# A gated-linear-attention loop on Trainium2: where GpSimd multiplies the keys and queries by their decay, and the order of products in the first late gate tile

## The chip, the cores and the metric

The kernel runs on one core of a Trainium2 chip. Its engines work side by side and meet by semaphores: TensorE (PE, matrix products into PSUM), VectorE (DVE), ScalarE (ACT), GpSimd (POOL), and SyncE (SP), which issues the DMAs. The metric is the device time of one execution in microseconds (us), as the median of several runs.

## The reference, cut to what matters

The whole program is three blocks: a convolution mixer, a gated linear attention (GLA) over 1024 tokens and 16 meta tokens, and a second block with attention and a feed-forward part. The change lies in the GLA block, whose core is this:

```
def _gla_chunk_step(S, inp):
    qc, kc, vc, gc = inp
    bc = jnp.cumsum(gc, axis=1)
    o_inter = jnp.einsum('bthd,bhde->bthe', qc * jnp.exp(bc), S)
    ...
    att = jnp.einsum('bthd,bshd,btshd->bhts', qc, kc, decay)
    o_intra = jnp.einsum('bhts,bshe->bthe', att, vc)
    b_last = bc[:, -1]
    S_new = jnp.exp(b_last)[..., None] * S + jnp.einsum(
        'bshd,bshe->bhde', kc * jnp.exp(b_last[:, None] - bc), vc)
    return S_new, o_inter + o_intra
```

After the loop the outputs are normed per head and multiplied by `silu(r)`, where `r` is a part of the product `h @ w_in`; that product with its silu is called the gate here.

## The kernel before

Numbers are float32. A product that needs the accuracy is made of three products of split operands: each operand is cut into a high part and a low part (`xh`, `xl` for the activations, `wh`, `wl` for a weight unit of 256 columns), and high times high, high times low and low times high are added in PSUM. A tile of 128 tokens by 256 columns is 8 steps over the depth times 3 = 24 matmuls (`token_tile`, its matmuls are recorded at line 354).

The GLA loop runs over `TILES`: tile 0 has the 16 meta tokens, tiles 1 to 8 have 128 tokens each (`NX` is 8). One pass c of it, on each engine in the order in which that engine's program is written:

- **TensorE** (`gla_tensor`): gate products of tile c (line 1049, spread between the others), gate logits of tile c+1 (1021), the pair scores from `arg_a` and `arg_b` (1082), the diagonal scores of tile c+1 (1060), the transposition of the decayed keys of tile c+1 (`turn_keys`, 1030), then a wait for `att_ready`, and then the output products (1096 and 1097, the second from `q_decayed`) and the state products (1104).
- **VectorE** (`gla_vector`): the state update (1275), the masked diagonal (1248), the early gate (1195), then for tile c+1 `sums` (a minimum at 1206, four running sums at 1212, one per head, a small product at 1215) and `exponents(c+1, 0)`, eight differences into `arg_a` (1226 and 1227); then `weights` of tile c, seven predicated copies of the pair scores from PSUM into `att` under a mask that lies in SBUF (1236), whose end raises `att_ready`; then `exponents(c+1, 1)`, six differences into `arg_b`.
- **ScalarE** (`gla_scalar`): exponentials, silus, squares and copies. Exponentials of the decayed keys are at 1130 (they raise `kdec_exp`), those of `arg_a` and `arg_b` at 1138, that of the decayed queries at 1154 (raises `qdec_exp`), the soft part of the gate at 1119 to 1122; the squares of the outputs stand at 1149, and the copy of the outputs out of PSUM at 1185.
- **GpSimd** (`gla_pool`): multiplies what ScalarE has exponentiated by the keys and queries: `k_decayed` (one instruction, line 1291), the eight halves of `arg_a` and the six of `arg_b` (1298 and 1299), `q_decayed` (one instruction, line 1302).

Nothing plans this order: it is that of the code. An engine that waits for a semaphore holds up all that stands behind the wait on it.

After the loop comes the late gate (`gla_gate_tensor`): 16 tiles (`EARLY`) of the last two of four gate columns' units. Its first unit, `U_R[2]`, is loaded by a DMA that SyncE issues when the last pair scores are done; VectorE then makes the high part (line 341, raises `unit_hi`) and the low part (line 343, raises `unit_ready`). The tiles use PSUM banks 4 to 7 in turn, so tile q from the fourth on waits until ScalarE has read tile q-4 (`r_left`). ScalarE (`gla_gate_scalar`) takes the silu of each tile and between them casts the high parts of later weight units (`BETWEEN`), which GpSimd completes with the low parts (line 330).

Of the kernel before, what the change touches and what calls it, by code (L numbers as in the profile page):

```python
# [5 lines left out]
ALU = mybir.AluOpType  # L6
# [5 lines left out]
P = 128  # L12
D = 1024
SEQ = 1024
META = 16
T = META + SEQ
KT = D // P
NX = SEQ // P
# [7 lines left out]
UNIT = 256  # L26
GH, GK, GV = 4, 128, 256
# [9 lines left out]
TILES = [(0, META)] + [(META + P * j, P) for j in range(NX)]  # L37
# [9 lines left out]
U_R, U_GO = (U_GR, U_GR + 1, U_GR + 2, U_GR + 4), (U_GR + 3, U_GR + 5, U_GR + 6, U_GR + 7)  # L47
# [22 lines left out]
def hybrid_block(nc, I, out):  # L70
    ctx = ExitStack()
    with ctx:
        base = (nc.sbuf_base + 31) // 32 * 32

        def at(name, shape, off, dt=F32):
            return nc.alloc_sbuf_tensor_at(name, shape, dt, offset=base + off)

        def sem(name):
            return ctx.enter_context(nc.semaphore(name))
# [22 lines left out]
        xh = at("xh", [P, KT, T], A0, F32R)  # L102
        xl = at("xl", [P, KT, T], A0 + KT * T * 4, F32R)
# [4 lines left out]
        wh = [at(f"wh{s}", [P, KT, UNIT], o, F32R) for s, o in enumerate(SLOTS)]  # L108
        wl = [at(f"wl{s}", [P, KT, UNIT], o + SLOT // 2, F32R) for s, o in enumerate(SLOTS)]
# [19 lines left out]
        qk = at("qk", [P, 2 * GH, T], Z0)  # L129
# [8 lines left out]
        k_decayed = at("k_decayed", [P, GH, P], S0 + 2 * SLOT)  # L138
# [8 lines left out]
        q_decayed = at("q_decayed", [P, GH, P], W0 + 8192 + 2048)  # L147
# [72 lines left out]
        PS = ctx.enter_context(nc.psum_tensor("PS", [P, 8, 512], F32))  # L220
# [28 lines left out]
        raw_ready, unit_hi, unit_ready = sem("raw_ready"), sem("unit_hi"), sem("unit_ready")  # L249
# [120 lines left out]
        def token_tile(slot, c0, bank):  # L370

            return products([(xh[:, k, c0:c0 + P], xl[:, k, c0:c0 + P], wh[slot][:, k, :], wl[slot][:, k, :])
                             for k in range(KT)], [(0, UNIT)], lambda c, cn: PS[:, bank, 0:cn])
# [606 lines left out]
        r_tile, r_left, r_used = sem("r_tile"), sem("r_left"), sem("r_used")  # L980
        EARLY = 2 * NX
# [13 lines left out]
        def level_arg(l):  # L995
            return ARGS[l // 4][:, l % 4, :, :]
# [9 lines left out]
        def head_blocks(ap, l):  # L1006
            return ap.rearrange("p h (m e b) -> p h m e b", e=2, b=64 >> l)
# [276 lines left out]
            nc.gpsimd.tensor_tensor(x, x, qk[:, GH:, 0:META], ALU.mult).then_inc(kdec_ready, 1)  # L1284

        def gla_pool(pool):
            for c, (c0, n) in enumerate(TILES):
                q, k = qk[:, 0:GH, c0:c0 + n], qk[:, GH:, c0:c0 + n]
                if 0 < c < NX:
                    pool.wait_ge(kdec_exp, c + 1)  # L1290
                    nc.gpsimd.tensor_tensor(k_decayed[:, :, 0:n], k_decayed[:, :, 0:n], k, ALU.mult).then_inc(kdec_ready, 1)
                if c == 0:
                    continue
                for g, group in enumerate(GROUPS):
                    pool.wait_ge(arg_exp, 2 * (c - 1) + g + 1)
                    for l in group:
                        e, ql, kl = head_blocks(level_arg(l), l), head_blocks(q, l), head_blocks(k, l)
                        nc.gpsimd.tensor_tensor(e[:, :, :, 0, :], e[:, :, :, 0, :], kl[:, :, :, 0, :], ALU.mult)
                        last = nc.gpsimd.tensor_tensor(e[:, :, :, 1, :], e[:, :, :, 1, :], ql[:, :, :, 1, :], ALU.mult)
                    last.then_inc(arg_mul, 1)  # L1300
                pool.wait_ge(qdec_exp, c)
                nc.gpsimd.tensor_tensor(q_decayed[:], q_decayed[:], q, ALU.mult).then_inc(qdec_ready, 1)


        rstd_own, early_ready, gla_ready = sem("rstd_own"), sem("early_ready"), sem("gla_ready")
# [4 lines left out]
        def gla_gate_tensor(pe):  # L1310
            pe.wait_ge(att_ready, 2 * NX)
            pe.wait_ge(k_rows_done, NX)
            pe.wait_ge(r_left, EARLY)
            for q in range(EARLY):
                slot, j = divmod(q, NX)
                if j == 0:
                    pe.wait_ge(unit_ready, U_R[2 + slot] + 1)
                if q >= 4:
                    pe.wait_ge(r_left, EARLY + q - 3)
                token_tile(slot, META + j * P, 4 + q % 4).then_inc(r_tile, 1)  # L1320
# [1504 lines left out]
        @block.tensor  # L2825
        def _(pe):
            inputs_tensor(pe)
            conv_in_tensor(pe)
            conv_norm_tensor(pe)
            conv_out_tensor(pe)  # L2830
            gla_in_tensor(pe)
            gla_tensor(pe)
            gla_gate_tensor(pe)
            gla_out_tensor(pe)
            attn_in_tensor(pe)
            attn_tensor(pe)
            mix_out_tensor(pe)
            ffn_tensor(pe)
            final_tensor(pe)
# [33 lines left out]
        @block.gpsimd  # L2873
        def _(pool):
            consts_pool(pool)
            conv_in_pool(pool)
            conv_norm_pool(pool)
            conv_out_pool(pool)
            gla_in_pool(pool)
            gla_pool(pool)  # L2880
            gla_gate_pool(pool)
            gla_out_pool(pool)
            attn_in_pool(pool)
            attn_pool(pool)
            mix_out_pool(pool)
            ffn_pool(pool)
# [26 lines left out]
```

## Time and profile before

| what | value |
|---|---|
| median of 3 runs | 2242.12 us (2237.64 to 2244.78) |
| the profiled execution | 2243.53 us, of which 2241.8 us are the span from first to last instruction |
| TensorE busy, whole span | 2158.0 us (96%) |
| VectorE, ScalarE, GpSimd busy | 1291.3, 807.9, 1041.3 us (58%, 36%, 46%) |
| mean granted TensorE clock | 0.991 of 2.4 GHz |
| the GLA loop | about 642 to 832 us from the span's start |
| the late gate | about 832 to 882 us |

In rows of the timeline the first number is the start in us from the span's start, the second the length from the start of the first to the end of the last instruction of the row, then engine, line, operation, what is written and read, and the count. Brackets at a row's end give the idle time before it on its engine and what ended it. Instructions of one engine overlap a little at their ends, so a row of several is shorter than the sum of its parts. A window that begins within a run of like instructions shows them apart.

### The profile page before, as it was taken

The numbers are of one execution on the slowest core, as the hardware profiler recorded it, in microseconds if no ns is written. First come the engines' busy times: TensorE is split into PE (matmuls) and PEld (weight loads), VectorE is DVE, ScalarE is ACT, GpSimd is POOL, SyncE is SP. The second block draws the span as 40 slices with busy tenths as digits, with TensorE's granted clock in tenths as the row PEclk, the third lists the DMA queues.
The fourth block names the chain that finished last, engine by engine and source line by source line (L and its number), as shares of the span: only waits on it lengthen the run. The fifth ranks groups of instructions, "written<-read, shape, count | busy, mean of one in ns | idle before, by whom it ended". The sixth has DMA issues, their size and how long they took to land.

```text
span 2241.8 us, 31509 instructions
## 1 busy us (share of the span) xinstructions
PE 2158.0 (96%) x12156; PEld 1867.1 (83%) x12156; DVE 1291.3 (58%) x1661; ACT 807.9 (36%) x1313; POOL 1041.3 (46%) x720
## 2 busy tenths in 40 slices
PE   7999989999998989999998989999999999999898
PEld 6999967899998889888896668878888888888687
DVE  2899988710029875750005655676666666566753
ACT  3444543111137762220115764342222222222453
POOL 2789941052236646023276541055655555655600
PEclk9999999999999999999999999999999999999999
DMA  4111113311100013221202013211111111111421
GB/s 135 57 38 38 58 56 105 104 52 56 33 26 1 1 57 123 95 76 52 100 18 81 1 50 112 72 42 57 37 56 49 54 56 56 51 43 56 160 76 47
DMA packets 110603, 136.62 MB, mean 61 GB/s; under 512 B 6976, under 2 KB 92608, under 8 KB 110366
## 3 DMA queue, kind: packets, MB, share of 16 engines
q1 hardware_dynamic: 110494, 135.08, 18.3%
q8 instruction: 79, 1.29, 0.2%
q14 instruction: 30, 0.25, 0.0%
HBM read 118.26 MB, written 16.81 MB: 60 GB/s over the span
## 4 chain that ended last, share of the span: by engine, by line
PE 80%; DVE 9%; ACT 3%; POOL 3%; issue 3%; DMA 1%; SPq 0%; DVEq 0%; POOLq 0%; ACTq 0%
PE PS L354 48%; PE PS L2384 17%; PE PS L1724 3%; PE PS L394 2%; POOL side_sum L534 2%; PE PS L2107 1%; PE PS L1735 1%; PE PS L1764 1%; DVE att L1236 1%; PE PS L383 1%; PE PS L1444 1%; PE PS L1777 1%; DVE arg_b L1227 1%; DVE arg_a L1227 1%; DVE decay L1212 1%
## 5 line engine op out<-in xcount | busy, mean ns | idle before, releaser
L2573 DVE TENSOR_TENSOR ff_acc<-ff_acc,PS 128x512 f32<-128x512 f32 x336 | 226.2, 685 | 190.4 <-PE PS L354 189.8
L354 PE MATMUL PS<-xh,wh 128*128 128x352 f32 (+2 forms) x944 | 287.4, 336 | 5.1 <-DVE xl L449 4.0
L354 PE MATMUL PS<-xl,wh 128*128 128x352 f32 (+2 forms) x944 | 285.9, 334 | 0.0
L354 PE MATMUL PS<-xh,wl 128*128 128x352 f32 (+2 forms) x944 | 285.4, 334 | 0.0
L354 PE MATMUL PS<-wh,xh 128*128 128x256 f32 (+1 forms) x784 | 229.9, 318 | 4.2 <-DVE wl L343 2.8
L2309 POOL TENSOR_TENSOR xl<-raw,xh 128x512 fp32r<-128x512 f32 x120 | 163.9, 1374 | 139.5 <-ACT xh L2438 139.5
L354 PE MATMUL PS<-wl,xh 128*128 128x256 f32 (+1 forms) x784 | 228.6, 316 | 0.0
L354 PE MATMUL PS<-wh,xl 128*128 128x256 f32 (+1 forms) x784 | 228.1, 316 | 0.0
L577 DVE SCALAR_TENSOR_TENSOR PS<-glu,conv_vec,PS 128x1040 f32<-128x1040 f32 x184 | 225.7, 1292 | 0.8
L354 PEld LDWEIGHTS PS<-xh,wh 128*128 128x128 f32 x944 | 174.7, 188 | 13.2 <-issue 5.8
L354 PEld LDWEIGHTS PS<-xl,wh 128*128 128x128 f32 x944 | 174.4, 188 | 8.0
L354 PEld LDWEIGHTS PS<-xh,wl 128*128 128x128 f32 x944 | 174.4, 188 | 7.7
L335 POOL CAST wh<-raw 128x2048 fp32r<-128x2048 f32 x15 | 28.4, 1896 | 301.6 <-PE PS L354 149.7
L330 POOL TENSOR_TENSOR wl<-raw,wh 128x2048 fp32r<-128x2048 f32 x31 | 144.5, 4662 | 49.5 <-ACT wh L326 48.3
L354 PEld LDWEIGHTS PS<-wh,xh 128*128 128x128 f32 x784 | 146.9, 189 | 15.3 <-issue 5.2
L2438 ACT CAST xh<-raw 128x512 fp32r<-128x512 f32 x120 | 72.3, 619 | 236.6 <-PE PS L2384 141.7
L354 PEld LDWEIGHTS PS<-wh,xl 128*128 128x128 f32 x784 | 148.2, 189 | 10.6
L354 PEld LDWEIGHTS PS<-wl,xh 128*128 128x128 f32 x784 | 147.9, 189 | 10.7
L2301 POOL TENSOR_TENSOR raw<-raw 128x512 f32<-128x512 f32 x80 | 115.2, 1440 | 49.6 <-DMA raw<-in_w_ffn_up_dram 43.6
L354 PE MATMUL PS<-dnh,ffh 128*128 128x512 f32 x336 | 131.4, 391 | 3.1 <-POOL dnl L2314 2.7
L354 PE MATMUL PS<-dnh,ffl 128*128 128x512 f32 x336 | 131.0, 390 | 0.0
L354 PE MATMUL PS<-dnl,ffh 128*128 128x512 f32 x336 | 131.0, 390 | 0.0
(398 smaller groups left out, 4967.2 us busy)
## 6 DMA issues: line engine op xcount, KB each, us to landing
h_rows<-rows SPq DMA_DIRECT2D x24, 512.0 KB, 2.6
rows<-h_rows SPq DMA_DIRECT2D x24, 512.0 KB, 3.6
dn_raw<-in_w_ffn_down_dram SPq DMA_DIRECT2D x22, 512.0 KB, 3.5
raw<-in_gla_w_in_dram SPq DMA_DIRECT2D x10, 1024.0 KB
raw<-in_w_ffn_gate_dram SPq DMA_DIRECT2D x20, 512.0 KB
raw<-in_w_ffn_up_dram SPq DMA_DIRECT2D x20, 512.0 KB
raw<-in_conv_w_in_dram SPq DMA_DIRECT2D x16, 512.0 KB
raw<-in_w_in_dram SPq DMA_DIRECT2D x8, 1024.0 KB
```

The costliest lines, as they stand in the source:

```text
L330: nc.gpsimd.tensor_tensor(wl[slot][:], raw_of(u)[0][:], wh[slot][:].bitcast(F32), ALU.subtract).then_inc(unit_ready, 1)
L354: last = nc.tensor.matmul(out_of(c, cn), s, x[:, c0:c0 + cn], start=n == 0 and m == 0, stop=n == len(terms) - 1 and m == 2)
L394: last = nc.tensor.transpose(blocks(bank)[:, k, 0:rows], src[0:rows, k * P:(k + 1) * P], ident[0:rows, 0:rows])
L534: ins = nc.gpsimd.tensor_tensor(acc[:], acc[:], tap_part[n % 3][:], ALU.add)
L577: ins = nc.vector.scalar_tensor_tensor(out=acc[k % 2], in0=x, scalar=w, in1=acc[k % 2], op0=ALU.mult, op1=ALU.add)
L1227: last = nc.vector.tensor_tensor(e[:, :, 1, :], x[:, :, 1, :], ref, ALU.subtract)
L1724: return nc.tensor.matmul(out, x, w[:, k, cols], start=begin, stop=end)
L2301: nc.gpsimd.tensor_tensor(out, a, b, op).then_inc(pool_own.sem, 1)
L2309: nc.gpsimd.tensor_tensor(lo, OP_AT[o], hi.bitcast(F32), ALU.subtract).then_inc(unit_ready, 1)
L2384: ins = nc.tensor.matmul(PS[:, OP_BANK[o], :], s[:, k, :], x[:, k, :], start=k == 0 and m == 0, stop=k == 3 and m == 2)
L2438: nc.scalar.copy(ring(o)[0], OP_AT[o]).then_inc(unit_hi, 1)
L2573: nc.vector.tensor_tensor(x, x, PS[:, dn_bank(p, n), :], ALU.add).then_inc(dn_left, 1)
```

## The change

Two things. In the loop, GpSimd's order changes. The product of the decayed keys of tile c waits, beside `kdec_exp`, for `arg_ready`, which VectorE raises with the last of its eight `arg_a` differences of that tile. The product of the decayed queries of tile c-1 no longer stands at the end of its own pass but behind the keys' product of tile c. In the last pass there is no keys' product (only the queries' of tile 7 at its beginning), and the queries' of tile 8 follow behind the loop.

In the late gate, the first tile is written out by hand: 16 products that need only the high part of the weights, behind a wait for `unit_hi`, and then the 8 products with the low part, behind the wait for `unit_ready`. The other 15 tiles are as before.

```
         def gla_pool(pool):
+            def decayed_queries(c):
+                c0, n = TILES[c]
+                pool.wait_ge(qdec_exp, c)
+                nc.gpsimd.tensor_tensor(q_decayed[:], q_decayed[:], qk[:, 0:GH, c0:c0 + n], ALU.mult).then_inc(qdec_ready, 1)
+
             for c, (c0, n) in enumerate(TILES):
                 q, k = qk[:, 0:GH, c0:c0 + n], qk[:, GH:, c0:c0 + n]
-                if 0 < c < NX:
-                    pool.wait_ge(kdec_exp, c + 1)
-                    nc.gpsimd.tensor_tensor(k_decayed[:, :, 0:n], k_decayed[:, :, 0:n], k, ALU.mult).then_inc(kdec_ready, 1)
                 if c == 0:
                     continue
+                if c < NX:
+                    pool.wait_ge(kdec_exp, c + 1)
+                    pool.wait_ge(arg_ready, 2 * (c - 1) + 1)
+                    nc.gpsimd.tensor_tensor(k_decayed[:, :, 0:n], k_decayed[:, :, 0:n], k, ALU.mult).then_inc(kdec_ready, 1)
+                if c > 1:
+                    decayed_queries(c - 1)
                 for g, group in enumerate(GROUPS):
...
-                pool.wait_ge(qdec_exp, c)
-                nc.gpsimd.tensor_tensor(q_decayed[:], q_decayed[:], q, ALU.mult).then_inc(qdec_ready, 1)
+            decayed_queries(NX)
...
-            for q in range(EARLY):
+            pe.wait_ge(unit_hi, U_R[2] + 1)
+            first = slice(META, META + P)
+            for k in range(KT):
+                for x in (xh, xl):
+                    nc.tensor.matmul(PS[:, 4, 0:UNIT], x[:, k, first], wh[0][:, k, :], start=k == 0 and x is xh, stop=False)
+            pe.wait_ge(unit_ready, U_R[2] + 1)
+            for k in range(KT):
+                last = nc.tensor.matmul(PS[:, 4, 0:UNIT], xh[:, k, first], wl[0][:, k, :], start=False, stop=k == KT - 1)
+            last.then_inc(r_tile, 1)
+            for q in range(1, EARLY):
```

On GpSimd, between the last `arg_b` product of tile 1 and the first `arg_a` products of tile 2 there stand, before the change (lines of the kernel before):

```order
L1298 TENSOR_TENSOR arg_b<-arg_b,qk 128x256
L1299 TENSOR_TENSOR arg_b<-arg_b,qk 128x256
L1302 TENSOR_TENSOR q_decayed<-q_decayed,qk 128x512 [waits qdec_exp]
L1291 TENSOR_TENSOR k_decayed<-k_decayed,qk 128x512 [waits kdec_exp]
L1298 TENSOR_TENSOR arg_a<-arg_a,qk 128x4x64 [waits arg_exp]
```

and in the changed kernel, at the same place (its own lines, where 1299 is the keys' product, 1290 the queries' and 1306 and 1307 the others):

```order
L1306 TENSOR_TENSOR arg_b<-arg_b,qk 128x256
L1307 TENSOR_TENSOR arg_b<-arg_b,qk 128x256
L1299 TENSOR_TENSOR k_decayed<-k_decayed,qk 128x512 [waits arg_ready,kdec_exp]
L1290 TENSOR_TENSOR q_decayed<-q_decayed,qk 128x512 [waits qdec_exp]
L1306 TENSOR_TENSOR arg_a<-arg_a,qk 128x4x64 [waits arg_exp]
```

The two products have changed places, and both now stand behind the wait for `arg_ready`.

On GpSimd in the last pass of the changed kernel, between the products of tile 7 and those of tile 8, one instruction stands:

```order
L1306 TENSOR_TENSOR arg_b<-arg_b,qk 128x256
L1307 TENSOR_TENSOR arg_b<-arg_b,qk 128x256
L1290 TENSOR_TENSOR q_decayed<-q_decayed,qk 128x512 [waits qdec_exp]
L1306 TENSOR_TENSOR arg_a<-arg_a,qk 128x4x64 [waits arg_exp]
L1307 TENSOR_TENSOR arg_a<-arg_a,qk 128x4x64
```

Here the queries' product has kept its old place and waits only for `qdec_exp`.

On TensorE, from the last output product of the loop into the first late gate tile, there stand before the change (`wh_61` and `wl_67` are the high and low part of the unit):

```order
L1097 MATMUL PS<-state,q_decayed 128x256
L354 MATMUL PS<-wh_61,xh 128x256 [waits r_left,unit_ready,k_rows_done,att_ready]
L354 MATMUL PS<-wl_67,xh 128x256
L354 MATMUL PS<-wh_61,xl 128x256
L354 MATMUL PS<-wh_61,xh 128x256
L354 MATMUL PS<-wl_67,xh 128x256
```

and in the changed kernel:

```order
L1097 MATMUL PS<-state,q_decayed 128x256
L1325 MATMUL PS<-wh_61,xh 128x256 [waits r_left,unit_hi,k_rows_done,att_ready]
L1325 MATMUL PS<-wh_61,xl 128x256
...
L1325 MATMUL PS<-wh_61,xl 128x256
L1328 MATMUL PS<-wl_67,xh 128x256 [waits unit_ready]
L1328 MATMUL PS<-wl_67,xh 128x256 x7
```

The tile's first product has waited for `unit_ready` before; now only its seventeenth does.

## Rows read from the trace of the kernel before

**Rows 1.** What TensorE waited for in the GLA loop: total us, times, longest:

```profile
PE PS L1096 <- DVE att L1236: 12.0, 7, 2.4
```

**Rows 2.** Stretches: from:to, length, TensorE busy (instructions), granted clock, DMA:

```profile
703.42:725.10 21.68, 19.96 (x148) 1.00 0.00 1
790.15:810.75 20.60, 19.52 (x144) 1.00 0.00 1
835.00:836.00 1.00, 1.00 (x5) 1.00 (x6) 0.52 (x2) 0.98 (x3) 0.00 (x0) 0.50 0.05 8
```

**Rows 3.** Timeline, TensorE and ScalarE where pass 2 ends and tile 3's exponentials follow:

```profile
703.45 0.67 PE L1096 MATMUL PS<-v_rows,att 128*128 128x256 f32 x2 [1.70 <-DVE att L1236]
...
708.38 1.49 ACT L1138 ACTIVATE arg_b<-arg_b 128x1536 f32<-128x1536 f32 x1 [0.21 <-DVE arg_b L1227]
```

**Rows 4.** Timeline of VectorE, tile 3's differences into arg_a and what follows:

```profile
697.00 0.42 DVE L1226 TENSOR_TENSOR arg_a<-decay 128x256 f32<-128x256 f32 x1
697.34 1.51 DVE L1227 TENSOR_TENSOR arg_a<-decay 128x256 f32<-128x256 f32 x1
...
699.44 3.87 DVE L1236 COPY_PREDICATED att<-pair_mask,PS 128x256 f32<-128x256 int32 x7
703.34 0.58 DVE L1226 TENSOR_TENSOR arg_b<-decay 128x256 f32<-128x256 f32 x1
```

**Rows 5.** Timeline of GpSimd in the same pass:

```profile
693.25 1.38 POOL L1302 TENSOR_TENSOR q_decayed<-q_decayed,qk 128x512 f32<-128x512 f32 x1
697.27 1.29 POOL L1291 TENSOR_TENSOR k_decayed<-k_decayed,qk 128x512 f32<-128x512 f32 x1 [2.65 <-ACT k_decayed L1130]
701.54 0.73 POOL L1298 TENSOR_TENSOR arg_a<-arg_a,qk 128x256 f32<-128x256 f32 x1 [2.98 <-ACT arg_a L1138]
...
707.08 0.90 POOL L1299 TENSOR_TENSOR arg_a<-arg_a,qk 128x256 f32<-128x256 f32 x1
```

**Rows 6.** Timeline, VectorE's four running sums: tile 1's, then tile 3's apart:

```profile
642.30 1.37 DVE L1212 TENSOR_TENSOR_SCAN decay<-decay,soft 128x128 f32<-128x128 f32 x4 [1.99 <-ACT soft L1122]
...
692.80 0.77 DVE L1212 TENSOR_TENSOR_SCAN decay<-decay,soft 128x128 f32<-128x128 f32 x1 [1.23 <-ACT soft L1122]
...
693.49 1.42 DVE L1212 TENSOR_TENSOR_SCAN decay<-decay,soft 128x128 f32<-128x128 f32 x1
...
694.83 0.71 DVE L1212 TENSOR_TENSOR_SCAN decay<-decay,soft 128x128 f32<-128x128 f32 x2
```

**Rows 7.** Timeline, tile 8's differences, which have no keys' product, and TensorE's next wait:

```profile
806.38 0.42 DVE L1227 TENSOR_TENSOR arg_a<-decay 128x256 f32<-128x256 f32 x1
...
810.75 0.67 PE L1096 MATMUL PS<-v_rows,att 128*128 128x256 f32 x2 [1.07 <-DVE att L1236]
```

**Rows 8.** Timeline, predicated copies of tile 8 with and without GpSimd beside them:

```profile
822.69 1.87 DVE L1236 COPY_PREDICATED att<-pair_mask,PS 128x256 f32<-128x256 int32 x4 [2.71 <-PE PS L1082]
826.16 1.98 DVE L1236 COPY_PREDICATED att<-pair_mask,PS 128x256 f32<-128x256 int32 x3 [1.60 <-PE PS L1082]
...
822.26 1.27 POOL L1302 TENSOR_TENSOR q_decayed<-q_decayed,qk 128x512 f32<-128x512 f32 x1
```

**Rows 9.** Timeline of TensorE, last pair scores of tile 2 from arg_a:

```profile
693.38 1.00 PE L1082 MATMUL PS<-arg_a 128*128 128x64 f32 x8
```

**Rows 10.** Timeline, from the loop's last product into the first late gate tile:

```profile
832.56 2.29 DVE L343 TENSOR_TENSOR wl<-raw,wh 128x2048 fp32r<-128x2048 f32 x1
...
831.57 0.59 PE L1097 MATMUL PS<-state,q_decayed 128*128 128x256 f32 x2
835.00 0.55 PE L354 MATMUL PS<-wh,xh 128*128 128x256 f32 x1 [2.83 <-DVE wl L343]
...
837.69 0.34 PE L354 MATMUL PS<-wh,xh 128*128 128x256 f32 x1
...
839.05 0.28 PE L354 MATMUL PS<-wh,xl 128*128 128x256 f32 x1
```

**Rows 11.** Timeline of the late gate: GpSimd's low part of the second unit, ScalarE's silus:

```profile
850.37 4.80 POOL L330 TENSOR_TENSOR wl<-raw,wh 128x2048 fp32r<-128x2048 f32 x1
...
861.89 0.65 ACT L1336 ACTIVATE r_silu<-PS 128x256 f32<-128x256 f32 x2
...
881.97 0.38 ACT L1336 ACTIVATE r_silu<-PS 128x256 f32<-128x256 f32 x1 [2.46 <-PE PS L354]
```

## The prediction, written before the changed kernel was timed

> **What bounds the kernel now.** I read the chain of work that ended last first: outside the GLA loop it is TensorE nearly all the way, inside the loop it hardly touches TensorE. There it runs VectorE, ScalarE, VectorE, and TensorE waits for it once a pass. The list of waits says how much that is: 12.0 us in seven waits before the output products, all for the predicated copies [rows 1]. They are 2.4 us for tile 1, 1.7 for each of tiles 2 to 6, and 1.1 for tile 7 [rows 3, 7]; tile 8 has none. The stretches confirm it: a pass lasts 21.7 us and TensorE is busy for 19.96 of them [rows 2]. So no reordering on other engines can take more than about 1.7 us from such a pass; from there on TensorE is the bound.
>
> Then the timelines of VectorE and GpSimd, side by side. Of the eight differences into `arg_a`, seven take 0.42 us and one takes 1.51 [rows 4]. That one starts when GpSimd's keys' product runs (697.27 for 1.29 us) and ends just after it [rows 5]. The running sums show the same: four of them take 1.37 us when GpSimd is quiet (0.34 each), but for tile 3 the second starts at 693.49 and the third only at 694.83, 1.34 us later, while the queries' product runs from 693.25 to 694.63 [rows 5, 6]. Two VectorE instructions per pass are thus held back by one GpSimd instruction each. Both lie on the chain.
>
> **The keys' product.** Moved behind the differences it no longer holds one back: 1.51 - 0.42 = 1.09 us per pass, for tiles 2 to 7, six passes. Tile 1 has its differences long before the loop proper, with nothing waiting. The trace has the pass without this product: tile 8's differences run at 0.42 throughout, and the pass that contains them lasts 20.60 instead of 21.68 us, the wait of TensorE 1.07 instead of 1.70 [rows 2, 7]. That is 1.08 us, from the row itself.
>
> **The queries' product.** It leaves the place beside the running sums: 1.34 - 0.36 = 0.98 us per pass (the 0.36 from the two later sums, 0.71 together [rows 6]). The first sum keeps its delay, which comes from the last `arg_b` product. For tile 8's sums nothing changes: that pass has no keys' product, so the queries' product stays where it was.
>
> **What the new place costs.** From the end of the differences (call it X, 699.5 in the rows) GpSimd now runs 1.29 + 1.3 us and begins `arg_a` at about X + 2.7, where it began at X + 2.0 [rows 5]. VectorE is then in its seven copies (until X + 3.8). Beside copies I take the cost as zero: four copies took 1.87 us (0.47 each) with the queries' product beside the first of them, the same pace as in the other passes, and that product took 1.27 us, no longer than elsewhere [rows 8]. The last two copies take 0.74 each also where GpSimd is idle (three in 1.98 us) [rows 8], so that is their shape and no contention. The upper bound, if copies were held like differences, is 2.6 us a pass for the two products alone. Beginning `arg_a` 0.7 us later costs nothing on TensorE: GpSimd ends it about X + 9.3 (before: 707.98, X + 8.5 [rows 5]) and TensorE wants it after the outputs have been copied, about X + 12. Nor does it change `arg_b`: VectorE's six differences lie wholly beside `arg_a` products either way (from 703.34, with GpSimd at it until 708 [rows 4, 5]); 0.1 us either way. The added wait holds up only the two moved products and `arg_a`, which needs ScalarE's 1.92 us after the same signal anyway. TensorE wants the keys' product at about X + 1.6 and the queries' at X + 4.4; they are done at X + 1.4 and X + 2.7.
>
> A rule of the Trainium skill stands beside this. The page "SBUF — State Buffer", section "Who interferes with whom", says that VectorE and GpSimd share a pair of ports, that a VectorE instruction with two SBUF inputs contends with a GpSimd instruction that reads SBUF, and that the one which starts first holds it throughout. That fits the held difference and the held sum. It does not say whether a predicated copy, which has a mask in SBUF and its data in PSUM but keeps old values of its target, counts as one input or two. By the second reading the copies would be held and the time would be that of the third rival, 2254 us; by the first it would be the forecast's. The copies' pace in the rows speaks for the first.
>
> **The sum for the loop.** The VectorE and ScalarE chain of a pass becomes 21.67 - 1.09 - 0.98 = 19.60 us, TensorE's own work is 21.67 - 1.70 = 19.97. So TensorE becomes the bound, by 0.4 us. I looked for mixed rings that are longer. One goes from the output products over ScalarE's squares to the exponential of `arg_b`, which starts 4.9 us after the outputs begin and had 0.2 us of idle before it [rows 3]: 4.8 + (21.67 - 4.9 - 2.07) = 19.5. The other goes from tile c's pair scores from `arg_a` (done 694.38 [rows 9]) to the next differences into the same buffer; these start at 695.66 and now at 694.7, so 0.3 us is left; as a ring it is 19.4. Neither bites.
> - Tile 1: the chain is 2.0 us shorter, the wait was 2.4: 2.0.
> - Tiles 2 to 6: five times the whole wait, 1.70: 8.5.
> - Tile 7: chain as before, but started a little ahead: 0.1. Tile 8: none.
>
> Together 10.6 us. Bounds: 6.5 if only the keys' product counts (6 x 1.09), 12.0 if every wait goes.
>
> **The late gate tile.** Before, TensorE ended the loop at 832.16, waited until 835.00 for the low part, and then ran at the granted clock of 0.50, that is 1.2 GHz, for its first twelve products (0.213 us apart, until 837.69), then at 0.118 us apart, 2.4 GHz; the second tile began at 839.17 [rows 2, 10]. Now the high part is there at 832.56. Sixteen products of 0.118 us take until 834.6; the low part comes at 834.85, eight more start at 835.0 as before and take 0.94 us. The pauses are 0.5 us each; those of 1.7 us inside the loop left the clock at 1.00 in that pass [rows 2, 3], so I take 2.4 GHz throughout. The second tile begins at 835.95: 3.2 us earlier. If the clock fell all the same, 12 products at 0.213 us would make it 2.5; if all 24 ran slow, 1.4.
>
> Then, what is late next. The tiles follow one another every 2.84 us, and TensorE now reaches each 3.2 us earlier, while the loads and splits of the next units have not moved against the loop's end. Unit two is ready at 855.2 [rows 11]; tile 8 would start at 855.8, which still fits. Tile 10 needs the bank of tile 6, whose silu ends at 862.2, since it stands behind a cast that waits for a DMA [rows 11]; tile 10 began at 864.7 and would now be due at 861.5. It waits 0.75 us. The rest of the stage has more room, and ends 2.4 us earlier (last silu before at 881.97 [rows 11]). What follows is TensorE's chain again. I take 2.4, bounds 1.4 and 3.2.
>
> **Sum:** 10.6 + 2.4 = 13.0 us. The profiled execution took 2243.5 us, so 2230.5; it lies 1.4 above the median of the runs, so the median should be 2229.1 us, 0.6% less.
>
> **Rivals.**
> 1. *Only the keys' product was in the way.* The second running sum is slow for another reason, or the queries' product finds another victim: 6.5 us in the loop and 2.4 behind it, 2233.2. Against it stands that a sum is slow only while that product runs. Chance 0.13.
> 2. *The stall moves from the differences to the copies, by the two moved products only.* 2.5 us for 2.07 in six passes, +2.6, less 2.4 for the gate tile: 2242.3, no change. Against it the four copies in 1.87 us. Chance 0.08.
> 3. *The copies are held by every GpSimd product.* Then keys, queries and the first `arg_a` products alternate with the seven copies. Seven copies 3.8 us, plus 2.6 for two products, plus some 0.65 for each of four `arg_a` products: 9.0 us instead of 3.8; two of the `arg_b` differences then go free (-0.75). Per pass 5.2 - 0.75 - 2.07 = +2.4, in six passes 14.3, less 2.4: 2254. It decides as soon as a copy costs more than 2.07 us of stall per pass. Against it: the last two copies run beside `arg_a` now, at the pace they have alone. Chance 0.05.
> 4. The forecast: 0.74.
>
> **Range and chances.** A change below 0.3% (6.7 us) can't be told from none. The forecast's own bounds are 12.0 + 3.2 = 15.2 (2226.9) and 6.5 + 1.4 = 7.9 (2234.2); the runs before scatter by some 3 us around their median. So 2224.5 to 2235.5 us, which takes in the first rival and leaves 2 and 3 out. Faster by over 0.3%: the forecast (0.74) and nearly all of rival 1 (0.11), 0.85. Within 0.3%: 0.02 + 0.08 = 0.10. Slower: 0.05.
>
> **What the changed profile would show.** All eight differences into `arg_a` at 0.42 us in tiles 2 to 7. Running sums: one of 0.77, then three 0.36 apart, save tile 8's. Seven copies still 3.87. TensorE's waits for the copies down from 12.0 to under 1.5 us, a pass at 20.0 us. The first late product at about 0.5 us behind the loop's last, clock 1.00 in the tile, and one wait of some 0.8 us at tile 10. Wrong it is if copies take longer than 4 us, if the passes stay above 20.5 us with TensorE waiting (a ring that I missed), or if the clock shows 0.50 in the gate tile.

## The result: what was measured, and the profile after

The changed kernel took 2225.16 us (median of 5 runs, 2220.37 to 2226.04) beside 2242.12 us for the kernel before (5 runs, 2237.64 to 2245.97). The ratio is 0.992, with a 95% interval of 0.9907 to 0.9933. So it is faster, as forecast, but by 17 us where 13.0 were forecast. The median itself lies 0.7 us above the lower end of the range, 2224.5 us; the ratio, set against the median of before, gives 2224.2 us, 0.3 us below it. Two more groups of runs of the changed kernel were taken later. Over all groups together (55 runs of the kernel before, 17 of the changed one) the medians are 2240.8 and 2227.2 us, 13.7 us apart. What lay inside the two places that were changed came out at 14.3 us; the rest of the first comparison's gain lay elsewhere, as shown below.

The program is cut into three parts here, by events that every kernel here has: the **loop**, from the gate logits of tile 1 (line 1021) to the end of the last output product; the **gate stage**, from there to the start of the last silu of the gate; and **outside**, all else of the span.

| profiled execution | span | loop | gate stage | outside |
|---|---|---|---|---|
| before | 2241.8 | 194.4 | 49.8 | 1997.6 |
| changed | 2223.4 | 182.3 | 47.6 | 1993.5 |
| difference | 18.4 | 12.1 | 2.2 | 4.1 |

What TensorE waited for in the changed loop and at its end, total us, times, longest (before: [rows 1]):

```profile
PE PS L1096 <- DVE att L1236: 1.2, 2, 0.9
PE PS L1325 <- DVE wh L341: 0.7, 1, 0.7
```

Of the seven waits for the copies two are left, 0.3 us for tile 1 and 0.9 for tile 7. A stretch of one pass, TensorE alone, in the columns of [rows 2] (length, busy, clock):

```profile
703.00:722.70 19.70, 19.70 (x149) 1.00 0.00 1
```

TensorE is busy for the whole of it. The timeline of VectorE and GpSimd for tile 3, answering [rows 4 to 6]:

```profile
693.73 0.75 DVE L1212 TENSOR_TENSOR_SCAN decay<-decay,soft 128x128 f32<-128x128 f32 x1 [0.44 <-ACT soft L1122]
...
694.72 0.71 DVE L1212 TENSOR_TENSOR_SCAN decay<-decay,soft 128x128 f32<-128x128 f32 x2
...
697.22 0.42 DVE L1227 TENSOR_TENSOR arg_a<-decay 128x256 f32<-128x256 f32 x1
...
698.23 3.92 DVE L1236 COPY_PREDICATED att<-pair_mask,PS 128x256 f32<-128x256 int32 x7
...
698.45 1.30 POOL L1299 TENSOR_TENSOR k_decayed<-k_decayed,qk 128x512 f32<-128x512 f32 x1 [4.25 <-DVE arg_a L1227]
699.71 1.31 POOL L1290 TENSOR_TENSOR q_decayed<-q_decayed,qk 128x512 f32<-128x512 f32 x1
```

The four sums take 1.7 us in all instead of 2.75, the difference that took 1.51 us takes 0.42, and the seven copies take 3.92 us with both products beside them, against 3.87 before. The stall has not moved.

The first late gate tile, timeline of TensorE, answering [rows 10]:

```profile
823.89 0.35 PE L1325 MATMUL PS<-wh,xh 128*128 128x256 f32 x1 [0.71 <-DVE wh L341]
...
825.74 0.28 PE L1325 MATMUL PS<-wh,xl 128*128 128x256 f32 x1
826.12 1.21 PE L1328 MATMUL PS<-wl,xh 128*128 128x256 f32 x8
827.17 0.28 PE L354 MATMUL PS<-wh,xh 128*128 128x256 f32 x1
...
853.39 0.39 PE L354 MATMUL PS<-wh,xh 128*128 128x256 f32 x1 [0.53 <-ACT r_silu L1352]
```

From the second on the products stand 0.12 us apart, where the first twelve stood 0.213 us apart before. The granted clock does not fall there, and tile 10 waits for the silu of tile 6, as forecast.

### The profile page after: what moved, and what is told of

It is laid out like the page before. It is cut to its first block, busy times and chain, and to the rows that moved or that the text cites. A ratio compares the mean times of both kernels' runs of the same rounds, so it can differ in the third digit from the quotient of the medians.

```text
span 2223.4 us, 31516 instructions
## 1 busy us (share of the span) xinstructions
PE 2151.6 (97%) x12156; PEld 1862.9 (84%) x12156; DVE 1282.0 (58%) x1661; ACT 807.6 (36%) x1313; POOL 1041.3 (47%) x720
## 3 DMA queue, kind: packets, MB, share of 16 engines
q1 hardware_dynamic: 110494, 135.08, 18.4%
q8 instruction: 79, 1.29, 0.2%
## 4 chain that ended last, share of the span: by engine, by line
PE 83%; DVE 5%; POOL 3%; ACT 3%; issue 3%; DMA 1%; SPq 0%; POOLq 0%; ACTq 0%; DVEq 0%
PE PS L354 47%; PE PS L2400 17%; PE PS L1740 3%; PE PS L394 2%; POOL side_sum L534 2%; PE PS L2123 1%; PE PS L1751 1%; PE PS L1049 1%; PE PS L1082 1%; PE PS L1780 1%; PE PS L383 1%; PE PS L1460 1%; PE PS L1793 1%; POOL wl L330 1%; PE PS L1738 1%
## 5 line engine op out<-in xcount | busy, mean ns | idle before, releaser
L330 POOL TENSOR_TENSOR wl<-raw,wh 128x2048 fp32r<-128x2048 f32 x31 | 144.6, 4663 | 51.1 <-ACT wh L326 49.9
```

Of the source, the lines that this page charges most:

```text
L330: nc.gpsimd.tensor_tensor(wl[slot][:], raw_of(u)[0][:], wh[slot][:].bitcast(F32), ALU.subtract).then_inc(unit_ready, 1)
```

## The experiments

All were run with the kernel before beside them. A table of every profile stands at the end of this section.

### 1 and 2: each product moved alone

The keys' product alone:

```
                     pool.wait_ge(kdec_exp, c + 1)
+                    pool.wait_ge(arg_ready, 2 * (c - 1) + 1)
                     nc.gpsimd.tensor_tensor(k_decayed...
```

> Only the keys' product is moved behind the differences; the queries' product stays at the end of its pass, beside the running sums, and the late gate tile is as before. My theory (each moved product takes away the one delay that it caused, and TensorE is the bound only when both are gone): a pass of 20.6 us instead of 21.67, a TensorE wait of 0.6 us left in each of tiles 2 to 6, the loop (from the gate logits of tile 1 to the last output product) 6.5 us shorter than in the kernel before, the gate stage unchanged. Rival A (the whole gain comes from the keys' product, the queries' was not in the way): the loop is 12 us shorter. Rival B (the delay moves to the copies): seven copies take over 4.5 us and the loop is not shorter. The part of the program outside the loop and the gate stage: if the 4 us that it lost in the changed kernel came by chance, here it scatters by some 3 us either way.

Measured: loop 187.8 us, 6.5 shorter, and passes of 20.6 us. The waits left for tiles 2 to 6 are 0.63 us each. Ratio 0.9962 (0.9948 to 0.9976). Timeline for tile 3, VectorE, then TensorE's wait:

```profile
693.34 2.75 DVE L1212 TENSOR_TENSOR_SCAN decay<-decay,soft 128x128 f32<-128x128 f32 x4 [1.23 <-ACT soft L1122]
...
698.88 3.91 DVE L1236 COPY_PREDICATED att<-pair_mask,PS 128x256 f32<-128x256 int32 x7
...
702.94 0.67 PE L1096 MATMUL PS<-v_rows,att 128*128 128x256 f32 x2 [0.63 <-DVE att L1236]
```

The sums keep their 2.75 us. This is the term of 6 x 1.09 us to the tenth, and rivals A and B fall. One part of the expectation failed: the gate stage, not edited here, was 48.6 us and not 49.8. The clock stayed at 1.00 there; experiment 6 comes back to this.

The queries' product alone (shown against the changed kernel, with its `decayed_queries`; the late gate tile is as before):

```
                 if c < NX:
                     pool.wait_ge(kdec_exp, c + 1)
-                    pool.wait_ge(arg_ready, 2 * (c - 1) + 1)
                     nc.gpsimd.tensor_tensor(k_decayed...
                 if c > 1:
+                    if c < NX:
+                        pool.wait_ge(arg_ready, 2 * (c - 1) + 1)
                     decayed_queries(c - 1)
```

> Only the queries' product is moved: the keys' product comes when its exponentials are ready, as before, and the queries' of the tile before follows it behind a wait for the end of the differences; the late gate tile is as before. My theory: the second running sum falls from 1.34 to 0.36 us, the sixth difference still takes 1.5 us, a pass lasts 20.7 us, and the loop is 5.9 us shorter. Rival A (the queries' product was not in the way): loop not shorter, sum still 1.34 us. Rival B (delay moves to the copies): copies above 4.5 us.

Measured: loop 184.4 us, 10.0 shorter, not 5.9; ratio 0.996 (0.9944 to 0.9975). The expectation failed on the keys' product. Timeline of VectorE and GpSimd where the two met before:

```profile
713.52 0.42 DVE L1226 TENSOR_TENSOR arg_a<-decay 128x256 f32<-128x256 f32 x1
...
715.20 0.41 DVE L1227 TENSOR_TENSOR arg_a<-decay 128x256 f32<-128x256 f32 x1
715.53 0.42 DVE L1226 TENSOR_TENSOR arg_a<-decay 128x256 f32<-128x256 f32 x1
715.87 0.41 DVE L1227 TENSOR_TENSOR arg_a<-decay 128x256 f32<-128x256 f32 x1
...
715.44 2.00 POOL L1298 TENSOR_TENSOR k_decayed<-k_decayed,qk 128x512 f32<-128x512 f32 x1 [3.25 <-ACT k_decayed L1130]
```

Here the keys' product comes while VectorE is at its sixth difference, and it is GpSimd that waits: 2.00 us instead of 1.29, and no difference is held. In the kernel before it came 0.27 us after the fifth had started and took the sixth's place [rows 4, 5]; here it came 0.24 us after the sixth had started and lost to the seventh and the eighth. Tile 2 of the same execution still goes the old way, VectorE and GpSimd:

```profile
674.32 0.42 DVE L1226 TENSOR_TENSOR arg_a<-decay 128x256 f32<-128x256 f32 x1
674.66 1.50 DVE L1227 TENSOR_TENSOR arg_a<-decay 128x256 f32<-128x256 f32 x1
...
674.60 1.28 POOL L1298 TENSOR_TENSOR k_decayed<-k_decayed,qk 128x512 f32<-128x512 f32 x1 [2.65 <-ACT k_decayed L1130]
```

The other passes bear this out. In the traces of the kernel before, of this experiment and of experiment 4 there are 21 keys' products beside differences. Thirteen came 0.275 to 0.281 us after the start of the fifth difference, and the sixth took 1.50 to 1.52 us each time. Eight came 0.19 to 0.26 us after the start of the sixth, and the product took 1.99 to 2.04 us each time. So an arrival some 0.3 us later turns the collision round. Whether the distance from the running difference's start decides, by hundredths of a microsecond, or which difference is running, these traces can't tell: the two always changed together.

The first cause of the later arrival is the shorter sums: ScalarE's key exponentials no longer wait for them, as they are held by its own work before (they start at 714.08, 0.67 us after the sums' end; before, at 695.92, 0.37 us after it), so the product arrives later against the differences. This also says what the change's two moves are worth: the queries' alone gives 10.0 us of the loop's 12.1, the keys' alone 6.5, so their gains overlap.

### 3 and 4: the loop alone, the gate tile alone

Experiment 3 has `gla_pool` of the changed kernel and `gla_gate_tensor` of the kernel before, experiment 4 the other way round.

> Both products moved, the late gate tile as before. My theory: a pass of 19.70 us as in the changed kernel, because a wait of TensorE costs what the list of waits says (1.70) and about 0.27 us of drain and restart beside it; loop 12.1 us shorter, gate stage unchanged (49.8 us), TensorE at 1.2 GHz in its first gate tile. Rival (the 0.27 us came by chance or from the gate tile): passes of 19.97 us, loop 10.6 us shorter.

> The loop as before, only the first late gate tile is split into its sixteen high-part products and eight low-part ones. My theory: loop unchanged, second gate tile 3.1 us earlier than before against the loop's end, gate stage 2.2 us shorter, since 0.8 us is given back where tile 10 waits for its PSUM bank; clock 1.00 throughout the tile. Rival (the clock stayed up in the changed kernel only because the loop before it had no waits): clock 0.50 in the tile, gate stage at most 1.9 us shorter.

Measured, loop alone: loop 182.2 us, gate stage 50.0, outside 2002.8; ratio 0.9961 (0.9941 to 0.9981). The loop is 12.1 us shorter with the old tile too, so the forecast's 10.6 was short by 1.5 and the gate tile has no part in that. The median, though, was only 5.6 us below the kernel before.

Measured, tile alone: loop 194.3, gate stage 47.6 (2.2 shorter), outside 1998.8; ratio 0.9995 (0.9981 to 1.0009). TensorE's start into the tile:

```profile
835.57 0.36 PE L1318 MATMUL PS<-wh,xh 128*128 128x256 f32 x1 [0.61 <-DVE wh L341]
```

and the stretches around it (length, TensorE busy, granted clock):

```profile
834.00:836.00 2.00, 1.39 (x9) 1.00 0.95 391
836.00:838.00 2.00, 1.90 (x16) 1.00 0.02 6
```

The clock stays at 1.00 here with the old loop before the tile, so that rival falls. The 2.2 us stand in the trace and cannot be told from nothing by the median of 12 runs.

### 5, 9 and 10: the outside part

The loop alone being 10 us slower than the whole change, where the gate stage gives 2.2, made the outside part the open question: nothing in it was edited. Experiments 5 and 9 are the changed kernel again, 10 is the loop alone again.

> The changed kernel once more, beside the others of this group. The profiles so far give, for the program outside the loop and the gate stage, 1993.5 us for the changed kernel and 1996 to 2003 us for five others, the kernel before among them (1997.6). Theory (chance: that part has the same instructions, and its time depends on how long TensorE runs at 1.2 GHz after each of some pauses, which differs from execution to execution): the loop again 182.3 us, the gate stage 47.6 us, the outside part some 1997 us with a scatter of 3 us, and the median gain over the kernel before nearer to 14.3 us than to 17. Rival (the changed kernel has a shorter outside part by its own): outside part again below 1995 us and a gain of 17 us or more.

> The changed kernel a third time. So far it was 0.8% and then 0.47% faster than the kernel before, in two groups of runs. In ten profiles the part of the program outside the loop and the gate stage lasted 1993.5 to 2002.8 us, and followed the time for which the granted clock was 0.50 there (20 to 44 us in each). Theory (chance): loop 182.2 us and gate stage 47.6 us again, outside part in line with its slow time, that is about 1984 us plus 0.4 times the slow time, and a median about 14 us below the kernel before, give or take 3. Rival (the changed kernel as such shortens the outside part): outside part below 1994.5 us with little slow time, and the gain 16 us or more.

> Both products moved, the gate tile as before, a second time. The first time its profile showed an outside part of 2002.8 us with 44 us at 1.2 GHz, and its median was only 5.6 us below the kernel before although its loop was 12.1 us shorter. Theory (chance): loop 182.2 us again, outside part below 2000 us, median 10 to 14 us below the kernel before. Rival (without the new gate tile the later part meets the slow clock more often): median again less than 8 us below, outside part above 2000 us.

Measured: 2228.36 us and a ratio of 0.9953 (0.9938 to 0.9968) in experiment 5; 2227.48 us and 0.9934 (0.9913 to 0.9954) in 9; 2230.67 us and 0.9954 (0.9936 to 0.9971) in 10. The loop was 182.2 or 182.3 us each time. The outside part was 1996.2, 1993.5 and 1993.2 us: for the loop alone it fell from 2002.8 to 1993.2 with no edit in between. In experiment 9 it met the first condition of the rival too, below 1994.5 us, but the gain of 15.1 us stayed below the rival's 16. A stretch near the end of the same program, in two executions of the same kernel, the changed one, first and again (length, TensorE busy, granted clock):

```profile
2092.00:2112.00 20.00, 14.64 (x69) 1.00 0.08 27
```

```profile
2092.00:2112.00 20.00, 14.82 (x50) 0.74 0.08 27
```

and a stretch in the attention part, loop alone, against 0.94 in both executions above:

```profile
1310.00:1340.00 30.00, 26.82 (x136) 0.72 0.22 77
```

The clock falls to 0.50 after some pauses of TensorE in one execution and not in another. Over the twelve profiles the outside part follows the time with the clock at 0.50 there (the last few microseconds of the span left out) with a correlation of 0.98: 1983.8 us plus 0.41 us for each slow microsecond. The recorded mean clocks say the same: over 50 runs of the kernel before, a mean clock lower by 0.001 goes with 1.5 us more (correlation -0.88; 2234.7 us at 0.996, for instance, and 2248.3 at 0.989).

So the 4.1 us outside go with the clock: 13.6 us less of slow time at 0.41 would be 5.6. The groups of runs differ as well (17.0, 12.1, 15.1 us between medians), and by more than their scatter: the intervals of the first and of experiment 5 do not overlap, and each of the first group's 5 runs of the changed kernel is shorter than each of the 6 in experiment 5. This too goes with the clock, 0.9946 and 0.9918 in the mean, which at 1.5 us per 0.001 is 4 us of the 4.7 between the mean times. Why the first group had the higher clock isn't shown; the groups ran on different chips (8, 2 and 1, the first group's isn't recorded).

Does the change itself favour the higher clock? The profiles alone leave it open: the outside part of the eight with both products moved was 1993.2 to 1996.2 us save one of 2002.8, that of the four others 1996.2 to 1998.8. The runs speak against it: 56 runs of kernels with both products moved have a mean clock of 0.9917, and so have the 50 of the kernel before. A lasting gain or loss of more than some 1.3 us by the clock (twice the standard error of that difference, at 1.5 us per 0.001) would show there.

### 6: early products thrown away

```
-                    nc.tensor.matmul(..., start=k == 0 and x is xh, stop=False)
-            pe.wait_ge(unit_ready, U_R[2] + 1)
-            for k in range(KT):
-                last = nc.tensor.matmul(..., wl[0][:, k, :], start=False, stop=k == KT - 1)
-            last.then_inc(r_tile, 1)
-            for q in range(1, EARLY):
+                    nc.tensor.matmul(..., start=k == 0 and x is xh, stop=k == KT - 1 and x is xl)
+            for q in range(EARLY):
```

> The changed kernel, but the sixteen early high-part products are thrown away: the tile then does all its 24 products behind the wait for the low part, as in the kernel before. Tells the work moved forward from the clock kept up. Theory: half of the 3.1 us that the second tile comes earlier is work moved (16 products of 0.118 us, 1.9 us), the other 1.2 us is the clock (12 products at 0.213 instead of 0.118). So here the second tile starts 1.2 us earlier against the loop's end than before, the gate stage lasts 48.6 us, with no wait at tile 10. Rival (all of the gain is work moved; the clock would have been up anyway): gate stage 49.8 us, or clock 0.50 in the tile.

Measured: gate stage 48.45 us, 1.4 shorter than before and 0.9 longer than in the changed kernel. Stretches over the tile:

```profile
824.00:826.00 2.00, 1.90 (x16) 1.00 0.00 0
826.00:828.00 2.00, 2.00 (x20) 1.00 0.86 251
```

Set against the profile of before, keeping TensorE at work before the tile, with no use of what it computes, brings 1.4 us; the products moved forward bring the rest, of which part is given back at tile 10. That the 1.4 us are the clock's, the other executions of the old tile show. With the clock at 0.50 for 3.4 us behind the wait the gate stage was 49.8, 49.9 and 50.0 us (before, experiments 10 and 3), with 6.8 us of it 51.3 (experiment 2). In experiment 1 the clock did not fall, though TensorE had waited as long, and the stage was 48.6 us, like the 48.45 here. Its start into the tile and the stretch behind it:

```profile
830.14 0.36 PE L354 MATMUL PS<-wh,xh 128*128 128x256 f32 x1 [2.86 <-DVE wl L343]
```

```profile
830.00:834.00 4.00, 3.86 (x32) 1.00 0.69 214
```

So the old tile met the low clock in four executions of five; with products ahead of the wait for the low part, used or thrown away, none of seven did. What the new tile saves against the old one is 1.0 us where the clock stays up by itself and 3.8 where it falls for longest. Ratio to the kernel before 0.9955 (0.9941 to 0.997).

### 7 and 8: what was left

```
                 if c > 1:
+                    pool.wait_ge(arg_ready, 2 * (c - 1) + 1)
                     decayed_queries(c - 1)
```

> The changed kernel, and in the last pass the queries' product of tile 7 also waits for the end of the differences, so that it no longer runs beside the running sums of tile 8. Theory (each wait of TensorE that goes brings its listed length and 0.25 us more): second running sum 0.36 us, the wait of 0.9 us for tile 7 gone, loop 1.1 us shorter than in the changed kernel, 181.1 us. Rival (the pass is bound elsewhere, as its keys' product is missing): loop 182.2 us.

Measured: loop 181.3 us, 1.0 shorter than in the changed kernel. The waits of its loop:

```profile
PE PS L1096 <- DVE att L1236: 0.3, 1, 0.3
```

A wait listed at 0.9 us went, and brought 1.0.

Experiment 8 has this and

```
-                   6: [(U_GO[2], GO_SLOTS[2])], 9: [(U_GO[3], GO_SLOTS[3])]}
+                   8: [(U_GO[2], GO_SLOTS[2])], 9: [(U_GO[3], GO_SLOTS[3])]}
```

> As the one before, and ScalarE's cast of the third output unit, which waits for its DMA and held up the silus of gate tiles 6 and 7, stands ahead of tile 8 instead of tile 6. Theory (the gate stage gave 0.8 us back at tile 10, which waited for the bank of tile 6): that wait disappears and the gate stage is 0.8 us shorter, 46.8 us. Rival (the low part of the unit then comes later and the end of the stage waits for it or for VectorE): 47.6 us or more.

Measured: gate stage 46.6 us, 0.95 shorter than in 7, with no wait for a silu in the list. Where that wait stays it isn't of one size: in experiment 9, the same code as the changed kernel, it was four times as long, and the gate stage 48.9 us:

```profile
PE PS L354 <- ACT r_silu L1352: 2.0, 1, 2.0
```

since the cast in front of silu 6 waits for a DMA. Experiments 7 and 8 have medians of 2228.91 and 2227.59 us and ratios of 0.9952 (0.9937 to 0.9967) and 0.9954 (0.9937 to 0.997); the changed kernel in the same group had 0.9953. Their 1.0 and 2.0 us are in the trace, and below what these runs can tell.

### All profiles

| kernel | loop | gate stage | outside | outside, clock at 0.50 |
|---|---|---|---|---|
| before | 194.4 | 49.8 | 1997.6 | 34.0 |
| changed | 182.3 | 47.6 | 1993.5 | 20.4 |
| 1 keys only | 187.8 | 48.6 | 1996.2 | 30.6 |
| 2 queries only | 184.4 | 51.3 | 1996.4 | 30.6 |
| 3 loop only | 182.2 | 50.0 | 2002.8 | 44.3 |
| 4 tile only | 194.3 | 47.6 | 1998.8 | 37.4 |
| 5 changed again | 182.2 | 47.6 | 1996.2 | 30.6 |
| 6 products thrown away | 182.4 | 48.5 | 1995.0 | 27.2 |
| 7 queries of tile 7 too | 181.3 | 47.6 | 1993.8 | 27.2 |
| 8 cast after tile 7 | 181.2 | 46.6 | 1993.9 | 23.8 |
| 9 changed a third time | 182.3 | 48.9 | 1993.5 | 23.8 |
| 10 loop only again | 182.2 | 49.9 | 1993.2 | 23.8 |

## Why the prediction was right in its mechanism and short in its size

- **What bounds the loop.** Right in kind: the loop's gain came from TensorE's waits for the copies, and with both products moved TensorE is busy all through a pass.
- **The keys' product, 1.09 us a pass.** Right, 6.5 us by itself in experiment 1.
- **The queries' product, 0.98 us a pass.** Right for the sums: 2.75 us became 1.70. The prediction added the two products' costs; in experiment 2 the shorter sums alone also undid the keys' collision, in tiles 3 to 7. The sum for both was not hurt by this, as TensorE's own work set the pass.
- **The copies cost nothing.** Right, 3.92 against 3.87 us. The rule cited from the Trainium skill ("SBUF — State Buffer", "Who interferes with whom") left open whether a predicated copy counts as two inputs from SBUF; in this trace it isn't held beside a GpSimd product. Rivals 2 and 3 fall. Rival 1 falls by the sums and by the pass of 19.70 us, where the keys' product alone left 20.6 (experiment 1).
- **TensorE's own work, 21.67 - 1.70 = 19.97 us: the step that failed.** A pass takes 19.70. The list of waits gives 1.70 us, measured from the modelled end of the last product, but a pass without the wait is 1.97 shorter: the drain and restart around a wait, 0.27 us, went too. The traces show where most of it lies: without a wait an output product starts 0.16 us before the modelled end of the one before it, and the first two behind a wait take 0.67 us where two together otherwise take 0.59 [rows 3, 10]. Experiment 1 has the same 0.27: a wait of 0.63 left and a pass of 20.59. The five passes of the whole wait gave 9.8 us for the 8.5 of the sum, 1.3 of the 1.5 us by which 10.6 was short of 12.1; the pass of tile 7 gave most of the rest, 0.26 us for 0.1. The bound of 12.0 "if every wait goes", and the 1.7 us taken as the most that a pass could gain, were too low for the same reason: experiment 7, with all but 0.3 us of the waits gone, has 13.1.
- **The ring over VectorE.** 19.60 us by the prediction, which would leave it 0.1 us under 19.70. The trace shows a little more room: in tiles 2 to 6 of the changed kernel the copies end 0.46 to 0.51 us before the output products start, against 0.15 us where TensorE waits for them, so some 0.3 us. The pass is nearly balanced.
- **The late gate tile.** Right: 2.2 us for a forecast of 2.4, with the clock up, and the give-back at tile 10 where it was put (listed 0.5 us, 0.7 more than the usual distance between two products; 0.75 forecast). Part of the agreement is luck: the clock in the old tile differed from execution to execution, and against others of them the same new tile saves 1.0 to 3.8 us.
- **The range.** Its terms summed to at most 15.2 us, and I allowed some 2.4 us beside them for the scatter. Loop and gate stage gave 14.3, inside. The outside part, which the sum put at nothing, gave 4.1 more in the profile and about 3 between the medians. That is the second failure, and the larger part of the miss: 14.3 us alone would have stayed in the range. I had the scatter of runs in hand, 3 us around a median of three, and didn't ask where it comes from; the slow clock outside the changed stages (34 us of it in the profile of before) can move a median of five by as much as rival 1 would.

## What to carry to other kernels

- When two engines run side by side without a semaphore between them, compare the same instruction's duration in a pass with the other engine quiet and in one with it busy. What differs is a hidden wait, and a move of the other engine's instruction beside something it doesn't hold brings it back for nothing.
- Take the gain of a removed TensorE wait from the difference of pass lengths, not from the listed idle time; here 0.27 us more went in each pass whose wait disappeared whole.
- Cut both spans at common events before explaining a difference of some microseconds: what lies outside the edited part must be accounted for by something else, here by the granted clock.

## What the runs showed of the hardware that I had not expected

- Whether GpSimd's product holds VectorE's difference or the other way round changed with the product's arrival: 0.28 us into the fifth difference, the sixth took some 1.51 us (13 cases); 0.19 to 0.26 us into the sixth, the product took some 2.0 (8 cases).
- The clock was at 0.50 for 20 to 44 us outside the loop and gate stage, a time that differed between executions of the same kernel, and with it the outside part, where nothing was edited, went from 1993 to 2003 us (correlation 0.98 over twelve profiles).
- With sixteen products before the wait whose results are thrown away, the gate stage was 1.4 us shorter than in the profile of before, and as long as where the clock stayed up without them (48.45 and 48.6 us).
